# An encoder layer on one core: the first weight unit multiplied block by block over all token tiles, with constants and bias issued later

## The chip, the cores and the metric

The kernel runs on one core of one Trainium2 chip. The metric is the device time of one launch in microseconds (us), lower is better. It is the median of several runs of the same program.

## What is computed

The reference takes 768 tokens of width 1024 (256 of a prompt, 512 of a sample) through one encoder layer. The part that matters here is its beginning: a root-mean-square norm of the tokens, and one wide projection of the normed tokens into queries, keys, values and gates.

```python
def rms_norm(x, g):
    x32 = x.astype(jnp.float32)
    y = x32 * lax.rsqrt(jnp.mean(x32 * x32, axis=-1, keepdims=True) + EPS)
    return (y * g.astype(jnp.float32)).astype(x.dtype)

h = rms_norm(x, norm_g)
proj = h @ w_in
dq, dk, dv, nq, nk, nv, gates = jnp.split(proj, IN_SPLITS, axis=-1)
dq = rms_norm(dq.reshape(B, S, DIFF_HEADS, 2, DIFF_HEAD_DIM), diff_qn) * (DIFF_HEAD_DIM ** -0.5)
```

After it come differential attention, neighbourhood attention, a gated merge with an output projection, a second norm, and a mixture of 16 experts (each picks 96 tokens) whose weights make up most of the bytes that are read.

## The kernel before

**Tiles and stages.** The 768 tokens are 6 tiles of 128 (`t`, `NT = 6`), the width of 1024 is 8 blocks of 128 (`k`, `KD = 8`). The program goes through the stages one after the other: `pd` (projection to the differential attention's queries, keys, values), the attention itself, `pn` and its attention, `g` (gates and branches), `o` (output), the routing, the experts. A stage's projection is cut into chunks of 512 output columns (queries, keys, values for `pd`), and a chunk into weight units of 4 blocks by 512 columns, 1 MB each. The first chunk (queries) is units 0 and 1.

**High and low parts.** Every fp32 operand is split into a rounded part ("high", made by ACT) and the rest ("low", made by DVE), and every product is three matmuls (lines 492 to 494, `split_product`): high tokens by high weights, high tokens by low weights, low tokens by high weights. A unit takes 6 tiles x 4 blocks x 3 = 72 matmuls of 512 columns on PE.

**The start.** SP issues, in this order: tokens turned to blocks 0 to 3 (`xT`, two transfers of 768 KB, line 334), unit 0 (`w_raw`, 1 MB, line 330), blocks 4 to 7, unit 1, and then the tokens once more, not turned (`x`, six transfers of 512 KB, line 337). Meanwhile ACT's queue issues the vectors (`rows`: norm gains), the constants (`cst`: identity for the transposes, the exponents for the power) and the lambdas, and POOL's queue issues two tables of attention bias. ACT makes `hT_high` of each block (line 860) and `w_high` of each unit (line 851). DVE makes `hT_low` (line 1133) and `w_low` (line 1113). PE's first matmul waits for the first 4 token blocks, for the whole of unit 0, and for the constants.

**The norm.** The tokens go into the projection without their row norm, which is put on later. ACT squares and sums each row of `x` (line 867, six tiles), DVE makes the mean (line 1129), zeroes two key tiles (line 1142) and multiplies the lambda vectors (lines 1145 and 1148). ACT takes the exponent of the lambda sums (line 872) and only then enters the stage's body, where it first makes unit 2's `w_high`, then squares each projected tile (line 877). DVE makes unit 2's `w_low` before it reduces those squares (line 1160). POOL takes the power -0.5 (line 390) and DVE writes the scaled queries `qn` (line 1176).

**The order on PE.** It is written out: for each step (chunk, unit, tile) 12 matmuls, and two steps after a tile of queries or keys is complete, 4 transposes of it (line 501) that wait for its `qn`. Unit 1's tile 0 is the first complete one, so the first transposes stand behind unit 1's tile 2.

```python
                    while jt < len(done_at) and n >= done_at[jt] + 2:
                        if jt == 0 and before is not None:
                            pe.wait_ge(S(before, "out"), len(ATT[before]))
                        pe.wait_ge(S(stage, "qn"), jt + 1)
                        transposes(stage, jt, qn[:, jt % 2, :], "tr")
```

A unit's raw buffer, one of two, is loaded again once DVE has split it. ACT splits unit n once PE has finished unit n - 2.

Of the kernel before, what the change touches and what calls it, by code (L numbers as in the profile page):

```python
# [24 lines left out]
P = 128  # L25
# [3 lines left out]
NT = N // P  # L29
KD = D // P  # L30
# [23 lines left out]
ACT = mybir.ActivationFunctionType  # L54
# [59 lines left out]
def encoder(nc, x_prompt, x_sample, x_turned, w_in, vectors, lambdas, bias_diff, bias_prompt, bias_sample, w_branch_diff, w_branch_na,  # L114
            w_out, norm2_g, w_expert_gate, w_expert_up, w_expert_down, consts, y_prompt, y_sample):
    ctx = ExitStack()
    with ctx:
# [6 lines left out]
        def sem(name):  # L124
            return ctx.enter_context(nc.semaphore(name))
# [110 lines left out]
        s_x = [sem(f"x_loaded{t}") for t in range(NT)]  # L236
        s_xT = [sem(f"xT_loaded{i}") for i in range(4)]
        s_cst = sem("constants_loaded")
        s_lamv = sem("lambdas_loaded")
        s_kz = sem("keys_zeroed")  # L240
# [78 lines left out]
        def _(sp):  # L319
# [11 lines left out]

            for u in range(2):
                for i in (2 * u, 2 * u + 1):
                    sp.dma_start(xT[:, 2 * i:2 * i + 2, :], x_turned[:, 2 * i:2 * i + 2, :]).then_inc(s_xT[i], 16)
                load_unit(u, src_of("pd", "q", u))
            for t in range(NT):
# [39 lines left out]
        def _(pool):  # L376
            def load_bias(nh):
# [4 lines left out]
                pool.dma_start(BIAS[nh][4], BIAS[nh][3]).then_inc(s_b[b], 16)  # L382

            load_bias(0)
            load_bias(1)
            pool.wait_ge(s_cst, 32)

# [97 lines left out]
        def _(pe):  # L485
            mm = nc.tensor.matmul

            pe.sem_inc(x_used, SPLITS)
            pe.wait_ge(s_cst, 32)
            def split_product(out, sh, sl, mh, ml, first, last):  # L490
# [35 lines left out]
            def project(stage, before):  # L526

                chunks = [c for c in CHUNKS if c[0] == stage]
                steps = chunk_steps(chunks)
                def bank_free(c, t):  # L530
                    if c > 0:
                        pe.wait_ge(S(stage, "pused"), NT * (c - 1) + t + 1)
                    elif before is not None:
                        after_attention(before, t)
                    elif t == 0:
                        pe.wait_ge(S("n1", "tev"), 4)

                done_at, jt = [], 0
                for n, (c, u, t) in enumerate(steps):
                    if before is None and (c, u, t) == (0, 1, 0):  # L540
                        pe.wait_ge(S("n1", "tev"), KD)
                    if before is None or n >= START_EARLY:
                        chunk_product(chunks, c, u, t, hTh, hTl, bank_free)
                    if u == 1 and c < 2:
                        done_at.append(n)
# [5 lines that stand above are left out]
                        jt += 1  # L551
# [286 lines left out]
        def _(act):  # L838
# [3 lines left out]
            def split_units(upto):  # L842

                while unit[0] < min(upto, UNITS):
                    n = unit[0]
                    act.wait_ge(w_loaded[n % 2], 16 * (n // 2 + 1))
                    if n >= OUT + 2:
                        act.wait_ge(s_phd, 6)
                    elif n >= 2:
                        act.wait_ge(w_prod, NT * (n - 1))  # L850
                    a_(split_slot(n)[0], wraw[:, n % 2], ACT.Copy).then_inc(w_high, 1)  # L851
                    unit[0] += 1

            for dst, src in ((rows, vectors), (cst, consts)):
                act.dma_start(dst, src).then_inc(s_cst, 16)
            act.dma_start(lamv, lambdas).then_inc(s_lamv, 16)
            act.wait_ge(s_cst, 32)
            for k in range(KD):
                act.wait_ge(s_xT[k // 2], 16)
                a_(hTh[:, k, :], xT[:, k, :], ACT.Copy, scale=g1[:, k:k + 1]).then_inc(S("n1", "high"), 1)  # L860
                if k % 4 == 3:
                    split_units(k // 4 + 1)
            for t in range(NT):
# [237 lines left out]
        def _(dve):  # L1101
# [13 lines left out]
            def split_units(upto):  # L1115

                while unit[0] < min(upto, UNITS):
                    n = unit[0]
                    dve.wait_ge(w_high, n + 1)
                    high, lows = split_slot(n)  # L1120
                    low(lows, wraw[:, n % 2], high).then_inc(w_split, 1)
                    unit[0] += 1


            dve.sem_inc(x_split, RAWS - 1)
            dve.wait_ge(s_cst, 32)

# [3 lines left out]
            for k in range(KD):  # L1131
                dve.wait_ge(S("n1", "high"), k + 1)
                v.scalar_tensor_tensor(hTl[:, k, :], xT[:, k, :], g1[:, k:k + 1], hTh[:, k, :].bitcast(F32), ALU.mult,
                                       ALU.subtract).then_inc(S("n1", "tev"), 1)
                if k % 4 == 3:
                    split_units(k // 4 + 1)
            dve.wait_ge(S("n1", "sq"), NT)
# [3 lines left out]
            for r in range(2):  # L1141
                v.memset(kT[r][64 * (1 - r):64 * (2 - r)], 0.0).then_inc(s_kz, 1)
            dve.wait_ge(s_lamv, 16)
            for m in range(2):
# [449 lines left out]
```

## Time and profile before

| What | Before |
|---|---|
| Median of 3 runs | 2252.39 us (2251.98 to 2252.77) |
| Profiled execution, its own time | 2251.67 us |
| Span of its profile | 2249.9 us |
| PE busy | 2158.8 us, 96% of the span |
| DVE, ACT, POOL busy | 71%, 61%, 8% of the span |
| Bytes moved | 624 MB, 277 GB/s over the span |

The span is what the profile covers of one execution, from its first instruction to its last; the execution's own time is 1.8 us longer. Busy shares are averages over stages that have different limits: the experts, from about 750 us on, fill most of the span. A change of the first tens of microseconds has to be read in that stretch, by what each engine waits for there.

### The profile page before, as it was taken

The page shows a single profiled execution, that of the slowest core. Times are in us where ns is not written, and L with a number is a line of the kernel's source. Part 1 is how long each engine was busy: PE and PEld are TensorE (multiplying, and loading weights), DVE is VectorE, ACT ScalarE, POOL GpSimd, SP SyncE. Part 2 cuts the span into 40 slices and gives each one's busy share as a digit, 9 for nine tenths or more (in the row PEclk, how much of TensorE's full clock was granted, in tenths as well). Part 3 has the DMA queues.
Part 4 walks back from the last instruction along what each step waited for, and adds up shares of the span by engine and source line. Part 5 has one row for each costly group of instructions (what it writes and reads, how often), then busy time and mean ns, then how long its engine had stood idle before and what let it go on. Part 6 is the DMA issues. An engine that isn't in the chain of part 4 may idle for free.

```text
span 2249.9 us, 30606 instructions
## 1 busy us (share of the span) xinstructions
PE 2158.8 (96%) x11924; PEld 1878.6 (83%) x11924; DVE 1590.0 (71%) x1288; ACT 1379.6 (61%) x1118; POOL 183.4 (8%) x140
## 2 busy tenths in 40 slices
PE   6999979999995999999999999999999999999997
PEld 5867868888775998899988899898998989999896
DVE  5366334323437888888888888888888888888885
ACT  5365425222224777777777767777776777777774
POOL 2102200000013000010100101010010100101010
PEclk9999989999996999999999999999999999999999
DMA  5110142113415999999999999999999999999994
GB/s 228 58 54 26 38 137 73 61 70 113 162 57 202 358 376 361 375 371 374 367 374 372 369 375 372 368 376 362 381 369 366 383 352 382 367 374 371 366 379 173
DMA packets 71582, 623.99 MB, mean 277 GB/s; under 512 B 8336, under 2 KB 8720, under 8 KB 18800
## 3 DMA queue, kind: packets, MB, share of 16 engines
q1 hardware_dynamic: 63264, 595.62, 68.6%
q0 software_dynamic: 7840, 27.40, 4.3%
q8 instruction: 30, 0.49, 0.1%
q10 hardware_dynamic: 432, 0.34, 0.0%
q14 instruction: 16, 0.13, 0.0%
HBM read 609.70 MB, written 13.63 MB: 277 GB/s over the span
## 4 chain that ended last, share of the span: by engine, by line
PE 84%; DVE 5%; ACT 4%; issue 3%; DMA 3%; POOL 0%; SPq 0%; ACTq 0%; DVEq 0%; POOLq 0%
PE PS L492 26%; PE PS L494 26%; PE PS L493 26%; DVE x_w_low L1113 2%; ACT x_w_high L1046 2%; PE PS L573 2%; PE PS L832 1%; PE PS L588 1%; DMA bias_windows<-in_bias_prompt 1%; PE PS L501 1%; DMA w_raw<-in_w_in 1%; DVE hidden L1471 1%; PE PS L601 1%; ACT w_high L851 1%; PE PS L699 0%
## 5 line engine op out<-in xcount | busy, mean ns | idle before, releaser
L1113 DVE TENSOR_TENSOR x_w_low<-x_w_raw,x_w_high 128x2816 fp32r<-128x2816 f32 (+1 forms) x382 | 1176.7, 3090 | 243.7 <-ACT x_w_high L1046 242.3
L1046 ACT ACTIVATE x_w_high<-x_w_raw 128x2816 fp32r<-128x2816 f32 (+2 forms) x384 | 979.1, 2557 | 252.1 <-PE PS L494 207.0
L492 PE MATMUL PS<-x_w_high,xT_high 128*96 128x352 f32 x2048 | 667.4, 326 | 1.4 <-DVE xT_low L1113 1.4
L494 PE MATMUL PS<-x_w_high,xT_low 128*96 128x352 f32 x2048 | 660.2, 322 | 0.0
L493 PE MATMUL PS<-x_w_low,xT_high 128*96 128x352 f32 x2048 | 657.9, 321 | 0.0
L492 PEld LDWEIGHTS PS<-x_w_high,xT_high 128*96 128x96 f32 x2048 | 330.2, 161 | 6.8 <-issue 4.4
L493 PEld LDWEIGHTS PS<-x_w_low,xT_high 128*96 128x96 f32 x2048 | 332.5, 162 | 2.4
L494 PEld LDWEIGHTS PS<-x_w_high,xT_low 128*96 128x96 f32 x2048 | 331.7, 162 | 1.5
L492 PE MATMUL PS<-x_w_high,hidden_high 128*96 128x512 f32 x704 | 280.0, 398 | 2.3 <-DVE x_w_low L1113 1.0
L493 PE MATMUL PS<-x_w_low,hidden_high 128*96 128x512 f32 x704 | 278.2, 395 | 0.0
L494 PE MATMUL PS<-x_w_high,hidden_low 128*96 128x512 f32 x704 | 277.9, 395 | 0.0
L492 PE MATMUL PS<-w_high,hT_high 128*128 128x512 f32 x528 | 212.5, 402 | 17.1 <-DVE w_low L1113 17.1
L494 PE MATMUL PS<-w_high,hT_low 128*128 128x512 f32 x528 | 207.3, 393 | 0.0
L493 PE MATMUL PS<-w_low,hT_high 128*128 128x512 f32 x528 | 206.7, 392 | 0.0
L492 PEld LDWEIGHTS PS<-x_w_high,hidden_high 128*96 128x96 f32 x704 | 113.9, 162 | 55.6 <-issue 9.7
L851 ACT ACTIVATE w_high<-w_raw 128x2048 fp32r<-128x2048 f32 x26 | 49.7, 1913 | 175.4 <-PE PS L494 172.2
L1113 DVE TENSOR_TENSOR w_low<-w_raw,w_high 128x2048 fp32r<-128x2048 f32 x26 | 59.6, 2292 | 136.8 <-ACT w_high L851 136.5
L494 PEld LDWEIGHTS PS<-x_w_high,hidden_low 128*96 128x96 f32 x704 | 113.3, 161 | 47.9
L493 PEld LDWEIGHTS PS<-x_w_low,hidden_high 128*96 128x96 f32 x704 | 113.6, 161 | 43.5
L454 POOL DMA_INDIRECT gathered<-t_dram,idxi x17 | 44.8, 2635 | 1200.6 <-PE PS L778 1194.9
L492 PEld LDWEIGHTS PS<-w_high,hT_high 128*128 128x128 f32 x528 | 100.1, 190 | 36.0 <-issue 17.1
L494 PEld LDWEIGHTS PS<-w_high,hT_low 128*128 128x128 f32 x528 | 99.7, 189 | 21.8
(183 smaller groups left out, 1775.4 us busy)
## 6 DMA issues: line engine op xcount, KB each, us to landing
x_w_raw<-in_w_expert_gate SPq DMA_DIRECT2D x128, 1408.0 KB, 8.4
x_w_raw<-in_w_expert_up SPq DMA_DIRECT2D x128, 1408.0 KB, 8.9
x_w_raw<-in_w_expert_down SPq DMA_DIRECT2D x96, 1536.0 KB, 8.4
x_w_raw<-in_w_expert_down SPq DMA_DIRECT2D x32, 1024.0 KB, 7.0
w_raw<-in_w_in SPq DMA_DIRECT2D x20, 1024.0 KB, 4.8
x<-in_x_sample SPq DMA_DIRECT2D x8, 512.0 KB, 13.6
bias_windows<-in_bias_sample POOLq DMA_DIRECT2D x8, 512.0 KB, 3.9
w_raw<-in_w_out SPq DMA_DIRECT2D x4, 1024.0 KB, 5.0
```

Of the source, the lines that this page charges most:

```text
L454: pool.indirect_dma_start(xe, None, t_dram, bass.IndirectOffsetOnAxis(ap=idxi[:, col:col + 1], axis=0)).then_inc(S("x", "xe"), 16)
L492: mm(out, sh, mh, start=first, stop=False)
L493: mm(out, sh, ml, start=False, stop=False)
L494: return mm(out, sl, mh, start=False, stop=last)
L501: i = nc.tensor.transpose(PS[:, 6 + jt % 2, c * P:(c + 1) * P], src[:, c * P:(c + 1) * P], ident)
L573: i = mm(PS[:, nm * (step % ring) + m, 0:nt * P], queries, keys, start=True, stop=True)
L588: i = mm(PS[:, 6 + a % 2, 0:w], turned[:, a % 2, c * P:(c + 1) * P], values[:, h * w:(h + 1) * w], start=c == 0, stop=c == nt - 1)
L601: i = nc.tensor.transpose(PS[:, 4 + a % 2, c * P:(c + 1) * P], maps[:, a % 4, 0, c * P:(c + 1) * P], ident)
L832: i = nc.tensor.transpose(PS[:, 6 + u % 2, f * CAP:(f + 1) * CAP], hid[:, (f0 + f) * P:(f0 + f + 1) * P], ident[0:CAP, 0:CAP])
L851: a_(split_slot(n)[0], wraw[:, n % 2], ACT.Copy).then_inc(w_high, 1)
L1046: a_(xh[:, w % SPLITS, 0:n], xraw[:, w % RAWS, 0:n], ACT.Copy).then_inc(x_high, 1)
L1113: return v.tensor_tensor(out, src, high.bitcast(F32), ALU.subtract)
```

## The change

SP now issues the vectors first, then for each of the first four blocks one transfer of its tokens (384 KB) and one of its part of unit 0 (256 KB), then blocks 4 to 7, unit 1 and `x` as before. ACT and DVE split each of the four blocks as it arrives, tokens and weights in turn. PE multiplies unit 0 with the block as the outer loop and all 6 tiles inside, into 6 banks of PSUM; the 72 matmuls are the same ones. POOL issues the constants and lambdas once DVE has made the low part of block 3, and the two bias tables once it has made that of block 7. From unit 1 on, the program is as it was.

```diff
-            for u in range(2):
-                for i in (2 * u, 2 * u + 1):
-                    sp.dma_start(xT[:, 2 * i:2 * i + 2, :], x_turned[:, 2 * i:2 * i + 2, :]).then_inc(s_xT[i], 16)
-                load_unit(u, src_of("pd", "q", u))
+            sp.dma_start(rows, vectors).then_inc(s_rows, 16)
+            first = src_of("pd", "q", 0).rearrange("p (k c) -> p k c", k=4)
+            for k in range(4):
+                sp.dma_start(xT[:, k, :], x_turned[:, k, :]).then_inc(S("n1", f"xT_loaded{k}"), 16)
+                sp.dma_start(wraw[:, 0, k], first[:, k]).then_inc(S("n1", f"w_loaded{k}"), 16)
+            for i in range(2, 4):
+                sp.dma_start(xT[:, 2 * i:2 * i + 2, :], x_turned[:, 2 * i:2 * i + 2, :]).then_inc(s_xT[i], 16)
+            load_unit(1, src_of("pd", "q", 1))
...
+            pool.wait_ge(S("n1", "tev"), 4)
+            pool.dma_start(cst, consts).then_inc(s_cst, 16)
+            pool.dma_start(lamv, lambdas).then_inc(s_lamv, 16)
+            pool.wait_ge(S("n1", "tev"), KD)
             load_bias(0)
             load_bias(1)
-            pool.wait_ge(s_cst, 32)
+            pool.wait_ge(s_cst, 16)
...
-            pe.wait_ge(s_cst, 32)
...
-                    elif t == 0:
-                        pe.wait_ge(S("n1", "tev"), 4)
+
+                if before is None:
+
+                    for k in range(4):
+                        pe.wait_ge(S("n1", "tev"), k + 1)
+                        pe.wait_ge(S("n1", "w_low"), k + 1)
+                        for t in range(NT):
+                            i = split_product(PS[:, t, :], hTh[:, k, t * P:(t + 1) * P], hTl[:, k, t * P:(t + 1) * P],
+                                              wh[:, 0, k], wl[:, 0, k], k == 0, False)
+                            if k == 3:
+                                i.then_inc(w_prod, 1)
+                    pe.wait_ge(s_cst, 16)
...
-                    if before is None or n >= START_EARLY:
+                    if n >= (NT if before is None else START_EARLY):
                         chunk_product(chunks, c, u, t, hTh, hTl, bank_free)
...
-            for dst, src in ((rows, vectors), (cst, consts)):
-                act.dma_start(dst, src).then_inc(s_cst, 16)
-            act.dma_start(lamv, lambdas).then_inc(s_lamv, 16)
-            act.wait_ge(s_cst, 32)
+            act.wait_ge(s_rows, 16)
             for k in range(KD):
-                act.wait_ge(s_xT[k // 2], 16)
+                act.wait_ge(*((S("n1", f"xT_loaded{k}"), 16) if k < 4 else (s_xT[k // 2], 16)))
                 a_(hTh[:, k, :], xT[:, k, :], ACT.Copy, scale=g1[:, k:k + 1]).then_inc(S("n1", "high"), 1)
-                if k % 4 == 3:
-                    split_units(k // 4 + 1)
+                if k < 4:
+                    act.wait_ge(S("n1", f"w_loaded{k}"), 16)
+                    a_(wh[:, 0, k], wraw[:, 0, k], ACT.Copy).then_inc(S("n1", "w_high"), 1)
+            unit[0] = 1
+            split_units(2)
...
-                if k % 4 == 3:
-                    split_units(k // 4 + 1)
+                if k < 4:
+                    dve.wait_ge(S("n1", "w_high"), k + 1)
+                    low(wl[:, 0, k], wraw[:, 0, k], wh[:, 0, k]).then_inc(S("n1", "w_low"), 1)
+            dve.wait_ge(S("n1", "w_low"), 4)
+            dve.sem_inc(w_split, 1)
+            unit[0] = 1
+            split_units(2)
```

How the order moves, at three places. In these rows a name stands for a tile, `out<-in`, with the shape, and a wait is named by its semaphore.

On SP, the head of its queue (transfers in the order in which it issues them). Before:

```order
L334 DMA xT<-in_x_turned 128x1536 x2
L330 DMA w_raw<-in_w_in 128x2048
L334 DMA xT<-in_x_turned 128x1536 x2
L330 DMA w_raw<-in_w_in 128x2048
L337 DMA x<-in_x_prompt 128x1024 x2
L337 DMA x<-in_x_sample 128x1024 x4
```

And of the change:

```order
L333 DMA rows<-in_vectors 128x152
L336 DMA xT<-in_x_turned 128x768
L337 DMA w_raw<-in_w_in 128x512
L336 DMA xT<-in_x_turned 128x768
L337 DMA w_raw<-in_w_in 128x512
L336 DMA xT<-in_x_turned 128x768
L337 DMA w_raw<-in_w_in 128x512
L336 DMA xT<-in_x_turned 128x768
L337 DMA w_raw<-in_w_in 128x512
L339 DMA xT<-in_x_turned 128x1536 x2
L331 DMA w_raw<-in_w_in 128x2048
L342 DMA x<-in_x_prompt 128x1024 x2
```

The same bytes stand ahead of `x` on this queue, but for the vectors, which come new from ACT's queue.

On PE, the first unit. Before, one wait stands ahead of all 72 matmuls:

```order
L484 UNCONDITIONAL_BRANCH [waits barrier_Pool_Activation_PE_DVE_SP_release]
L492 MATMUL PS<-w_high,hT_high 128x512 [waits n1_tev,unit_split_ready,constants_loaded]
L493 MATMUL PS<-w_low,hT_high 128x512
L494 MATMUL PS<-w_high,hT_low 128x512
L492 MATMUL PS<-w_high,hT_high 128x512
```

In the change, such a wait stands ahead of every 18 matmuls (`n1_tev` counts low parts of token blocks, `n1_w_low` those of weight blocks); here the end of the first block and the start of the second:

```order
L502 MATMUL PS<-w_high,hT_low 128x512
L500 MATMUL PS<-w_high,hT_high 128x512
L501 MATMUL PS<-w_low,hT_high 128x512
L502 MATMUL PS<-w_high,hT_low 128x512
L500 MATMUL PS<-w_high,hT_high 128x512 [waits n1_w_low,n1_tev]
L501 MATMUL PS<-w_low,hT_high 128x512
```

The first matmul no longer waits for the constants nor for blocks 1 to 3.

On PE, the first transposes of queries (`cst` holds the identity), of the change:

```order
L500 MATMUL PS<-w_high,hT_high 128x512
L501 MATMUL PS<-w_low,hT_high 128x512
L502 MATMUL PS<-w_high,hT_low 128x512
L509 MATMUL PS<-cst,qn 128x128 [waits pd_qn]
L509 MATMUL PS<-cst,qn 128x128 x3
L500 MATMUL PS<-w_high,hT_high 128x512
L501 MATMUL PS<-w_low,hT_high 128x512
```

Before, the same rows stand at the same place, behind 108 matmuls (lines 492 to 494 and 501); nothing moved here.

## Rows read from the trace of the kernel before

**Rows 1.** The page's chain that ended last: shares of the span by engine.

```profile
PE 84%; DVE 5%; ACT 4%; issue 3%; DMA 3%; POOL 0%; SPq 0%; ACTq 0%; DVEq 0%; POOLq 0%
```

**Rows 2.** Waits of PE, 0 to 60 us: total us, times, longest us.

```profile
PE PS L492 <- DVE w_low L1113: 17.1, 1, 17.1
PE PS L501 <- DVE qn L1176: 0.3, 1, 0.3
```

**Rows 3.** The chain in order of time, 0 to 60 us: start us, us, what.

```profile
3.69 15.34 DMA w_raw<-in_w_in
19.05 1.92 ACT w_high L851
...
27.07 1.16 ACT junk L867 x2
...
29.12 2.62 DVE kT L1142
...
32.43 2.62 DVE kT L1142
...
35.78 1.91 ACT w_high L851
...
37.82 2.29 DVE w_low L1113
...
41.00 1.66 POOL small L390
...
42.69 0.76 DVE qn L1176
```

**Rows 4.** Timeline, 0 to 18 us: start, us, engine, line, what [idle before <-releaser].

```profile
5.46 1.28 ACT L860 ACT_TABLE_LOAD   x1 [5.46 <-DMA xT<-in_x_turned]
9.48 3.41 ACT L860 ACTIVATE hT_high<-xT,rows 128x768 fp32r<-128x768 f32 x4 [2.74 <-DMA cst<-in_consts]
10.54 3.80 DVE L1133 SCALAR_TENSOR_TENSOR hT_low<-xT,rows,hT_high 128x768 fp32r<-128x768 f32 x4 [10.54 <-ACT hT_high L860]
12.80 1.89 ACT L851 ACTIVATE w_high<-w_raw 128x2048 fp32r<-128x2048 f32 x1
...
14.73 2.29 DVE L1113 TENSOR_TENSOR w_low<-w_raw,w_high 128x2048 fp32r<-128x2048 f32 x1 [0.39 <-ACT w_high L851]
...
17.12 0.76 PE L492 MATMUL PS<-w_high,hT_high 128*128 128x512 f32 x1 [17.12 <-DVE w_low L1113]
```

**Rows 5.** Loads of `x` (line 337): issue durations ns, first and last issue; time to landing.

```profile
L337 SPq DMA_DIRECT2D x<-in_x_sample x4: 445/1252/2259, 5.2 to 8.5; - x4
L337 SPq DMA_DIRECT2D x<-in_x_prompt x2: 461/464/467, 4.2 to 4.7; - x2
...
DMA to landing us min/median/max: 16.1/17.9/19.2
```

**Rows 6.** The load of `x` issued last, at 8.5 us: KB, us to landing.

```profile
x<-in_x_sample SPq DMA_DIRECT2D x1, 512.0 KB, 18.2
```

**Rows 7.** All transfers between 2 and 27 us.

```profile
DMA packets 2371, 10.09 MB, mean 404 GB/s; under 512 B 272, under 2 KB 656, under 8 KB 2052
```

**Rows 8.** Timeline of PE at the first transposes of the `pd` stage.

```profile
43.49 0.65 PE L501 MATMUL PS<-cst,qn 128*128 128x128 f32 x4 [0.28 <-DVE qn L1176]
...
45.37 0.39 PE L492 MATMUL PS<-w_high,hT_high 128*128 128x512 f32 x1
```

**Rows 9.** Timeline of PE at the same place in the `pn` stage.

```profile
221.46 1.09 PE L501 MATMUL PS<-cst,qn 128*128 128x128 f32 x4 [3.08 <-DVE qn L1176]
...
224.88 0.39 PE L492 MATMUL PS<-w_high,hT_high 128*128 128x512 f32 x1
```

**Rows 10.** Stretches of 2 us: busy us by engine, granted TensorE clock, DMA share, GB/s.

```profile
221.00:223.00 2.00, 1.54 (x6) 1.47 (x7) 1.82 (x4) 0.41 (x1) 1.70 (x2) 0.60 0.60 250
...
225.00:227.00 2.00, 2.00 (x13) 1.65 (x12) 0.00 (x0) 0.54 (x1) 0.00 (x0) 1.00 0.04 8
```

**Rows 11.** A stretch in which `v_windows` loads (256 KB transfers, 2 KB pieces).

```profile
312.00:314.00 2.00, 0.90 (x3) 0.18 (x1) 0.13 (x1) 0.00 (x0) 0.00 (x0) 0.50 0.26 103
```

More of the change, by code:

```diff
@@ L236, in encoder @@
         s_x = [sem(f"x_loaded{t}") for t in range(NT)]
-        s_xT = [sem(f"xT_loaded{i}") for i in range(4)]
+        s_xT = {i: sem(f"xT_loaded{i}") for i in range(2, 4)}
         s_cst = sem("constants_loaded")
+        s_rows = sem("vectors_loaded")
         s_lamv = sem("lambdas_loaded")
@@ L845, in split_units @@
                     n = unit[0]
-                    act.wait_ge(w_loaded[n % 2], 16 * (n // 2 + 1))
+                    act.wait_ge(w_loaded[n % 2], 16 * ((n + 1) // 2))
                     if n >= OUT + 2:
@@ L1118, in split_units @@
                     n = unit[0]
-                    dve.wait_ge(w_high, n + 1)
+                    dve.wait_ge(w_high, n)
                     high, lows = split_slot(n)
@@ L1125, in _ @@
             dve.sem_inc(x_split, RAWS - 1)
-            dve.wait_ge(s_cst, 32)
+            dve.wait_ge(s_rows, 16)
             def mean_eps(out, in_, w, done):
@@ L1142, in _ @@
                 v.memset(kT[r][64 * (1 - r):64 * (2 - r)], 0.0).then_inc(s_kz, 1)
+            dve.wait_ge(s_cst, 16)
             dve.wait_ge(s_lamv, 16)
```

## The prediction

> **What bounds the kernel now.** I read the page's chain first: PE holds 84% of it [rows 1], so a start of PE that comes earlier shortens the whole run, as long as nothing else holds PE back afterwards. Then PE's waits in the first 60 us [rows 2]: there are only two, 17.1 us for the first weight unit's low part, and 0.3 us at the first transposes for the scaled queries `qn`. The first looks like the prize of this change. The second, small as it is, decides what the prize is worth, because it says that PE is not alone on the path at 43 us. So I read the chain in order of time [rows 3]: it does not run through PE's 26 us of matmuls at all. It runs from the load of unit 1 (landed at 19.05 us) to ACT's `w_high` of unit 1, six squares of `x` (the last starts at 27.07), two zeroings of key tiles on DVE (29.12 and 32.43), ACT's and DVE's split of unit 2 (35.78 and 37.82), POOL's power (41.00) and `qn` (42.69). Only then come the transposes, at 43.49 [rows 8]. Before the change, PE arrives 0.28 us ahead of that chain. The two are balanced almost to the microsecond, and the change speeds up only one of them.
>
> **PE's side.** Before, PE starts at 17.12 us, released by `w_low` [rows 4]. With blocks, it needs the first token and weight block alone. ACT's table load ended at 6.74 (5.46 + 1.28), and it hung on the first 768 KB of tokens, where now 384 KB and the vectors come first, so not later. Then a block's `hT_high` takes 3.41 / 4 = 0.85, its `hT_low` 3.80 / 4 = 0.95, and its `w_high` a quarter of 1.89, its `w_low` a quarter of 2.29 [rows 4] = 0.57. On the path lie 0.85, 0.95 and 0.57; `w_high`, 0.47, runs on ACT beside `hT_low`. PE starts at 6.74 + 2.37 = about 9.1 us, 8.0 us earlier.
>
> From start to transposes PE has 108 matmuls: 43.49 - 0.28 - 17.12 = 26.1 us, a slow start included [rows 4, 8]. A block of 18 is 4.3 us of that. It is fed in 384 + 256 KB at 404 GB/s [rows 7] = 1.6 us, and split in 1.3 us by ACT and 1.5 us by DVE, so the next block is always there. Unit 1 is needed 17.4 us after the start, at 26.5; even landing at 19.05 as before, with 1.92 and 2.29 behind it, it is ready by 23.3. So PE reaches the transposes at 9.1 + 26.1 = 35.2 us.
>
> **The norm's side.** What does the change do to `qn`? From the last square on, DVE's, ACT's and POOL's work is untouched and in the same order: 42.69 + 0.76 - 27.07 = 16.4 us [rows 3]. What could move is the squares. They need ACT free of unit 1's `w_high`, and `x`. ACT can be free earlier, since unit 1 lands earlier. But `x` cannot: the first of its six loads lands at 4.2 + 16.1 = 20.3, the last at 8.5 + 18.2 = 26.7 [rows 5, 6], 0.4 us before its square starts. The DMA engines are full all the way (404 GB/s over 2 to 27 us [rows 7]), and the bytes ahead of the last `x` tile stay the same: 5 MB of tokens and units, 3 MB of `x`, and the 1.3 MB of vectors, constants, lambdas and bias. All but the vectors POOL now issues in the middle of the stretch. Eight `hT_low` and four quarters of `w_low` take DVE 9.9 us from about 7.6, so the bias is issued near 17.5 and goes in between the tiles of `x`. So I take 0 for the move of `qn`, from the row it is nearest to, the landing of the last `x`.
>
> The bounds: if the bias slips behind `x` entirely, `x` comes 0.92 MB / 404 GB/s = 2.3 us earlier, and `qn` at most 2.3 + 0.4 = 2.7 us. In the other direction, pieces are shorter: 3 KB for token blocks, 2 KB for weight blocks, where 6 and 8 KB stood. `x` itself goes in 4 KB pieces at full rate [rows 5, 7]. The nearest row with 2 KB pieces is the load of `v_windows`, 103 GB/s [rows 11], though it reads another layout. If the 1.05 MB of weight blocks went at that rate, they would take 10.2 us and not 2.6, and `qn` would come 7.6 us late. I take the value near `x`.
>
> On this point the Trainium skill speaks against the change. The page DMA: Bandwidth & Descriptors, section Measured, says to batch transfers to 1 MiB or more for three quarters of the peak; its fit gives each transfer 2.0 us plus its bytes at 436 GB/s. By that, eight transfers of 384 and 256 KB cost 22 us where three larger ones cost 12, an estimate from that page, and the result would be some 10 us slower. The trace disagrees where transfers queue up: the six of 512 KB land 6.4 / 5 = 1.28 us apart [rows 5, 6], where the fit gives 3.2.
>
> **The other parts.** PE's wait for the constants now stands behind unit 0, at 26.5. They are issued when DVE has made four low parts, near 13.5, so nothing waits there. POOL's only other work in that time is the power at 41.00 [rows 3], and the bias is read in the attention, after all three chunks. The four extra waits on PE and the ten extra issues on SP (about 0.46 us each [rows 5]) cost nothing: SP is ahead of the DMA engines, which have work queued. If that cover were gone, ten issues would be 4.6 us.
>
> **What is late next.** PE reaches the transposes at 35.2 and waits to 43.5, 8.3 us, in place of 0.3. So the gain at the start is a wait at line 501, to the microsecond. And the wait has a price. In the `pn` stage PE already waits 3.08 us at the same line, and the granted clock is 0.60 of 2.4 GHz over the 2 us around the restart, that is 1.2 GHz for most of them, and 1.00 again from 225 us [rows 9, 10]. From the transposes' start to the seventh matmul behind them are 224.88 - 221.46 = 3.42 us there, and 45.37 - 43.49 = 1.88 us in `pd`, where PE had been busy [rows 8, 9]. The difference, 1.54 us, falls on PE just when PE is the bound again: it arrives at the second transposes later than their `qn`. Bounds: 0, if the clock is back by then, and 3.1, if it lasts twice as long.
>
> **The sum**, against the profiled execution: 2251.67 + 0 (move of `qn`) + 1.5 (clock) = 2253.2 us. That execution lies 0.7 us below the median, so the median goes to 2253.9 us, 0.07% more. A measurement of this kernel can tell about 0.2%, or 4.5 us, from no change. This is none.
>
> **The rivals.**
> - *The start counts in full.* If the transposes did not hold PE, the run would be 8.0 us shorter: 2244.4. For it speak the 17.1 us [rows 2] and PE's 84% [rows 1]; against it the chain [rows 3], which does not pass through PE before 43 us, and the unmoved order on PE. Chance 4%.
> - *The bias slips behind `x`.* `qn` 2.7 us earlier, clock lost: 2251.2, no change either. For it: POOL issues late. Against it: near 17.5 the last `x` tile is still 9 us off. 12%, inside the forecast's sign.
> - *The pieces are slow, and `x` comes late.* One mechanism, on the DMA queue of SP: the weight blocks at 103 GB/s push `x`, the squares and `qn` back 7.6 us, and with the clock the run is 9.1 us slower, 2261.5. It decides from 3.0 us on, when the 2.6 MB of the eight transfers take 9.5 us and not 6.5, a rate of 276 GB/s. For it: [rows 11]. Against: the full rate with `x` [rows 5, 7]. 8%. This is also the way in which the page's rule would work.
> - *The change doesn't do what it says*, PE not starting before some 15 us, since the blocks come in turn with other work. Then PE waits less at the transposes and keeps its clock: 2252.4. 6%.
>
> **How the numbers follow.** The forecast, the start's gain lost at the transposes, the norm's chain where it was, the clock paid: 70%. With the second and fourth rival, no measurable change has 0.88. Faster has the first rival and a little: 0.04. Slower has the third: 0.08. The range takes in the bounds of `qn` and the clock: from -2.7 + 1.5 = -1.2, and 1.0 less for a clock that costs less, 2250.2; up to 1.5 us of slower transfers with the long clock, +4.6, 2257.0. The far ends, 2244 and 2261, are left out.
>
> **What the profile after would show.** Right: PE's first matmul near 9 us; one wait of some 8 us of `L501`'s successor for `qn`, from about 35 to 43.5; a granted clock of about half in the 3 us behind it; the last square of `x` near 27, and the zeroings and `qn` where they were. Wrong: the last square before 24 or past 30, or transposes that start well before 43 us. The forecast falls if `x` lands at another time, or if PE's later stages give the time back.

## The result and the profile after

The changed kernel takes 2260.53 us (median of 6 runs, 2257.41 to 2262.31) where the kernel before takes 2252.47 us (6 runs). The ratio is 1.0032, 95% interval 1.0022 to 1.0042: 0.3% slower. On a second chip it was 1.0026 (1.0015 to 1.0036). I had forecast 2253.9 us and no measurable change.

The profiled execution took 2257.41 us, 5.7 us more than that of before. PE's waits in the first 60 us come first (total us, times, longest us):

```profile
PE PS L509 <- DVE qn L1200: 10.5, 1, 10.5
PE PS L500 <- DVE w_low L1131: 9.5, 1, 9.5
```

Line 509 is line 501 of before, where the wait was 0.3 us [rows 2]. PE starts at 9.5 us and not at 17.1, and all 7.6 us of that, and 2.6 more, are spent in front of the first transposes. The chain in order of time (start us, us, what) shows what it waits for:

```profile
10.27 19.39 DMA x<-in_x_sample
29.68 1.16 ACT junk L885 x2
...
31.73 2.62 DVE kT L1165
...
35.05 2.62 DVE kT L1165
...
38.40 1.90 ACT w_high L869
...
40.42 2.29 DVE w_low L1131
...
43.60 1.66 POOL small L399
...
45.28 0.76 DVE qn L1200
...
46.09 1.11 PE PS L509 x4
```

Against [rows 3] every step is there with its old duration, 2.6 us later. The chain now hangs on the last load of `x`, which lands at 29.66 us where it landed at 26.7 [rows 5, 6]. ACT waited for two tiles of `x` ahead of that (timeline of ACT, idle before and releaser at the end):

```profile
26.28 1.06 ACT L885 ACTIVATE junk<-x 128x1024 f32<-128x1024 f32 x1 [1.54 <-DMA x<-in_x_sample]
...
28.41 1.06 ACT L885 ACTIVATE junk<-x 128x1024 f32<-128x1024 f32 x1 [0.97 <-DMA x<-in_x_sample]
```

Then the clock, in stretches of 2 us (busy us by engine, granted clock, DMA share, GB/s):

```profile
44.00:46.00 2.00, 0.00 (x0) 0.00 (x0) 0.99 (x3) 0.30 (x1) 2.00 (x2) 0.50 0.85 319
46.00:48.00 2.00, 1.91 (x7) 1.72 (x8) 1.54 (x4) 0.69 (x1) 1.71 (x2) 0.50 0.41 172
48.00:50.00 2.00, 2.00 (x7) 1.53 (x6) 0.00 (x0) 0.00 (x0) 0.78 (x1) 0.51 0.00 0
50.00:52.00 2.00, 2.00 (x12) 1.69 (x11) 0.00 (x0) 0.66 (x2) 0.00 (x0) 1.00 0.00 0
```

PE works at 1.2 GHz for 3.9 us behind its wait. The same DVE instruction, compared in the two traces, is 2.6 us late before the transposes and 4.4 us late at 47.7 us of before (timelines of DVE, before and after):

```profile
47.66 0.69 DVE L1160 TENSOR_REDUCE small<-sq 128x8 f32<-128x512 f32 x1 [2.13 <-ACT sq L877]
```

```profile
52.06 0.69 DVE L1184 TENSOR_REDUCE small<-sq 128x8 f32<-128x512 f32 x1 [4.34 <-ACT sq L895]
```

The 1.8 us between are the clock. "Late at 47.7 us" stands for this comparison in what follows.

Why `x` lands late is in the first microseconds. The same view, in stretches of 1 us from 4 to 8 us, of before:

```profile
4.00:5.00 1.00, 0.00 (x0) 0.00 (x0) 0.00 (x0) 0.00 (x0) 0.00 (x0) 1.00 1.04 410
5.00:6.00 1.00, 0.00 (x0) 0.00 (x0) 0.00 (x0) 0.54 (x1) 0.00 (x0) 1.00 1.02 420
6.00:7.00 1.00, 0.00 (x0) 0.00 (x0) 0.00 (x0) 0.74 (x1) 0.00 (x0) 1.00 0.99 410
7.00:8.00 1.00, 0.00 (x0) 0.00 (x0) 0.00 (x0) 0.00 (x0) 0.00 (x0) 1.00 1.08 439
```

and after:

```profile
4.00:5.00 1.00, 0.00 (x0) 0.00 (x0) 0.00 (x0) 0.00 (x0) 0.00 (x0) 1.00 0.76 220
5.00:6.00 1.00, 0.00 (x0) 0.00 (x0) 0.00 (x0) 0.60 (x1) 0.00 (x0) 1.00 0.81 198
6.00:7.00 1.00, 0.00 (x0) 0.00 (x0) 0.00 (x0) 0.99 (x2) 0.00 (x0) 1.00 0.92 271
7.00:8.00 1.00, 0.00 (x0) 0.00 (x0) 0.25 (x1) 1.00 (x2) 0.00 (x0) 1.00 1.02 268
```

The engines are nearly as busy, and move little more than half as much. The trace's records of the single pieces say more. Of the 376 pieces of 2 and 3 KB in these 4 us, half take no more than 84 ns (2 KB) and 121 ns (3 KB), as between 8 and 12 us, where the rest of the eight transfers goes at 350 GB/s and more. But 61 of them take over twice that, together 20.8 of the 55.9 us that the 376 take on the 16 engines. Of the 235 pieces of 6 to 8 KB in the same 4 us of before, none does.

One more place lost time, far from the edit. POOL's 14 loads of bias windows in the neighbourhood attention run from the first to the last issue (timeline of POOL). Before:

```profile
307.74 0.60 POOL L382 DMA_DIRECT2D bias_windows<-in_bias_prompt  x1 [36.03 <-DVE small L1219]
...
363.97 0.53 POOL L382 DMA_DIRECT2D bias_windows<-in_bias_sample  x1 [3.67 <-DVE small L1219]
```

After:

```profile
310.47 0.60 POOL L387 DMA_DIRECT2D bias_windows<-in_bias_prompt  x1 [36.03 <-DVE small L1243]
...
368.05 0.53 POOL L387 DMA_DIRECT2D bias_windows<-in_bias_sample  x1 [3.67 <-DVE small L1243]
```

That is 56.2 us before and 57.6 after, though no instruction of it was changed.

### The profile page after: what moved, and what is told of

The parts are those of the page before. It is cut to its first block, busy times and chain, and to the rows that moved or that the text cites. A ratio compares the mean times of both kernels' runs of the same rounds, so it can differ in the third digit from the quotient of the medians.

```text
span 2255.6 us, 30622 instructions
## 1 busy us (share of the span) xinstructions
PE 2162.2 (96%) x11924; PEld 1881.6 (83%) x11924; DVE 1589.9 (70%) x1291; ACT 1380.4 (61%) x1121; POOL 181.6 (8%) x142
## 4 chain that ended last, share of the span: by engine, by line
PE 84%; DVE 5%; ACT 3%; issue 3%; DMA 3%; POOL 0%; SPq 0%; DVEq 0%; ACTq 0%; POOLq 0%
PE PS L500 26%; PE PS L502 26%; PE PS L501 25%; DVE x_w_low L1131 2%; ACT x_w_high L1064 2%; PE PS L591 2%; PE PS L606 1%; PE PS L850 1%; DMA x<-in_x_sample 1%; DMA bias_windows<-in_bias_prompt 1%; PE PS L509 1%; DVE hidden L1495 1%; PE PS L619 1%; DMA bias_windows<-in_bias_sample 0%; ACT w_high L869 0%
## 5 line engine op out<-in xcount | busy, mean ns | idle before, releaser
L1131 DVE TENSOR_TENSOR w_low<-w_raw,w_high 128x2048 fp32r<-128x2048 f32 (+1 forms) x29 | 60.1, 2071 | 137.8 <-ACT w_high L869 137.1
```

The costliest lines, as they stand in the source:

```text
L1131: return v.tensor_tensor(out, src, high.bitcast(F32), ALU.subtract)
```

## Experiments

Theory A: the small transfers run slow, so `x` and the norm's chain land late, and PE's long wait costs its clock. Theory B: the constants and bias, moved into the stretch of `x`, delay it. Theory C: the order by blocks costs PE time itself. All ratios are against the kernel before on the same chip, with their 95% intervals.

**The change again** (no edit).

> The changed kernel once more, on the chip of the next three. Both theories: 5 to 10 us over the kernel before; the last square of x near 29.7 us where it was 27.07, the first transposes near 46 us behind a wait of about 10 us, PE at half clock for some 3.8 us behind them. If the part of the loss that lies past 60 us is a matter of where the clock falls, the times scatter by some us and the granted clock of the runs goes with them.

Measured: 2259.74 us against 2253.07, ratio 1.0026 (1.0015 to 1.0036). Last square at 29.21, transposes at 45.63 behind a wait of 10.25 us, 4.1 us late at 47.7 us. The first 60 us repeat. The kernel before scattered from 2248.8 to 2257.1 us on this chip, so medians alone don't place a loss of 2 us. The profiles do.

**Three large transfers in place of eight.**

```diff
-            for k in range(4):
-                sp.dma_start(xT[:, k, :], x_turned[:, k, :]).then_inc(S("n1", f"xT_loaded{k}"), 16)
-                sp.dma_start(wraw[:, 0, k], first[:, k]).then_inc(S("n1", f"w_loaded{k}"), 16)
+            for i in range(2):
+                sp.dma_start(xT[:, 2 * i:2 * i + 2, :], x_turned[:, 2 * i:2 * i + 2, :]).then_inc(S("n1", f"xT_loaded{i}"), 16)
+            sp.dma_start(wraw[:, 0], first).then_inc(S("n1", "w_loaded0"), 16)
```

> The change with its first four blocks loaded in the three large transfers of before; everything else as changed. Theory A (the small transfers are slow in the first 9 us, so x and with it the norm land late): the last square of x starts at 27 to 27.5 again, the transposes at 43.5 to 44, and what is left over before is the clock, 1.5 to 2.5 us. Theory B (constants and bias, moved into the stretch of x, delay it): the last square stays near 29.7 and the time stays that of the change.

Measured: 2257.35 us, 1.0017 (1.0007 to 1.0027). The rate at 4 to 8 us is back (same view):

```profile
4.00:5.00 1.00, 0.00 (x0) 0.00 (x0) 0.00 (x0) 0.00 (x0) 0.00 (x0) 1.00 1.03 412
5.00:6.00 1.00, 0.00 (x0) 0.00 (x0) 0.00 (x0) 0.24 (x1) 0.00 (x0) 1.00 0.97 406
6.00:7.00 1.00, 0.00 (x0) 0.00 (x0) 0.00 (x0) 1.00 (x1) 0.00 (x0) 1.00 1.09 414
```

The last square and the transposes (timelines of ACT and PE):

```profile
26.34 1.06 ACT L885 ACTIVATE junk<-x 128x1024 f32<-128x1024 f32 x1
...
42.75 0.66 PE L509 MATMUL PS<-cst,qn 128*128 128x128 f32 x4 [4.16 <-DVE qn L1200]
```

Theory A holds, and B falls as a cause by itself: with constants and bias still issued late, the chain is even 0.7 us earlier than before. The 0.7 us are ACT's wait for unit 1, which lands at 16.7 us here and at 19.0 before (timelines of ACT, before and here, the squares right behind):

```profile
19.05 1.92 ACT L851 ACTIVATE w_high<-w_raw 128x2048 fp32r<-128x2048 f32 x1 [0.73 <-DMA w_raw<-in_w_in]
```

```profile
18.33 1.91 ACT L869 ACTIVATE w_high<-w_raw 128x2048 fp32r<-128x2048 f32 x1
```

At 47.7 us the kernel is 0.9 us late, which is the clock's 1.6 less that 0.7.

**Constants and bias at the start, small transfers kept.**

```diff
-            pool.wait_ge(S("n1", "tev"), 4)
-            pool.dma_start(cst, consts).then_inc(s_cst, 16)
-            pool.dma_start(lamv, lambdas).then_inc(s_lamv, 16)
-            pool.wait_ge(S("n1", "tev"), KD)
+            act.dma_start(cst, consts).then_inc(s_cst, 16)
+            act.dma_start(lamv, lambdas).then_inc(s_lamv, 16)
```

> The change with constants, lambdas and bias issued at the start, as before, and the small transfers kept. Theory A: the last square of x stays near 29 to 30.5 us, since the first microseconds carry the slow small transfers and the other bytes as well; time as the change within 1.5 us. Theory B: the last square comes back to about 27 us, transposes at 43.5, time 2.6 us under the change.

Measured: 2258.82 us, 1.0029 (1.0018 to 1.0041). Rates of 298, 257 and 277 GB/s between 5 and 8 us, last square at 29.64. A, against B. But here the squares wait for unit 1 and not for `x` (chain in order of time):

```profile
7.06 14.54 DMA w_raw<-in_w_in
21.62 1.92 ACT w_high L865
23.54 1.04 ACT junk L883 x2
```

Unit 1 lands 2.6 us later than before, and six squares follow without a gap. The slow transfers delay all that stands behind them on the queue, and whichever of unit 1 and `x` lands too late then holds the norm's chain.

**PE held back.**

```diff
+                    pe.wait_ge(S("n1", "tev"), KD)
                     for k in range(4):
```

> The change with PE held until all eight token blocks have their low part (about 19.4 us), so that it arrives at the transposes just when qn does. Theory A says that the wait of 10.5 us at the transposes costs its clock: with a wait of under 1.5 us PE keeps full clock there, and the run is about 1.8 us shorter than the change although PE starts 10 us later. Rival C (the order by blocks costs PE time itself, or an early start is worth something after all): the time is that of the change, or up to 9 us longer.

Measured: 2257.65 us, 1.0027 (1.0017 to 1.0037), which alone can't be told from the change. PE at the transposes, and the clock there (a stretch of 2 us):

```profile
46.36 0.66 PE L509 MATMUL PS<-cst,qn 128*128 128x128 f32 x4 [0.27 <-DVE qn L1201]
```

```profile
46.00:48.00 2.00, 1.73 (x10) 1.44 (x10) 1.42 (x4) 1.38 (x2) 1.30 (x2) 1.00 0.53 221
```

PE starts 10 us later than in the change, the transposes come 0.7 us later than in its repeat, and at 47.7 us the kernel is 2.9 us late and not 4.1. The early start is worth nothing, and the wait costs 1.9 us of clock. C falls.

**The small transfers alone, in the kernel before.** The same eight transfers, with PE's order, constants and bias as before.

> The kernel before with its first four token blocks and unit 0 loaded in the eight small transfers; order on PE, constants and bias as before. Theory A: 200 to 310 GB/s between 4 and 8 us where it was 410 to 440, last square of x near 29.5 to 30, transposes near 46, no wait over 1 us there, so no fall of the clock: 2.5 to 3.5 us slower in the first 60 us. If the pieces are not to blame: last square near 27, time as before. For the stretch from 300 to 365 us: longer by 1.3 us or more if five more transfers on SP's queue matter (as early_constants would have it, whose POOL list is that of before), as before within 0.3 us if only POOL's list does.

Measured: 2254.83 us against 2252.29, 1.0011 (1.0002 to 1.0021). 174 and 285 GB/s between 4 and 6 us, last square at 29.07, transposes at 46.44 with no wait for `qn`: PE itself started late, at 19.3, since unit 0 was late too. 2.9 us late at 47.7 us. The transfers account for 2.0 us of landing and 2.2 of PE's start. The rest is PE's slow pace behind its start: matmuls come 0.43 us apart for 5.5 us, before for 2.9, and 0.23 apart after that.

When the loads land, by kernel (issue plus time to landing, us; `late_on_pool` and `late_bias_on_before` are the kernel before with constants and bias, or the bias alone, issued late, see below):

| Kernel | Last load of the first four blocks | Unit 1 | Last `x` |
|---|---|---|---|
| before | 12.72 | 19.03 | 26.70 |
| the change | 12.72 | 19.18 | 29.66 |
| three large transfers | 10.43 | 16.67 | 25.37 |
| constants and bias at the start | 15.30 | 21.60 | 29.25 |
| small transfers on before | 14.76 | 21.03 | 28.71 |
| `late_on_pool` | 9.97 | 16.22 | 26.91 |
| `late_bias_on_before` | 10.45 | 16.71 | 25.24 |

So the eight transfers cost 2.0 us of landing in the kernel before, 2.3 us in the change, and 4.3 us at its last `x`. In the change this hides at first: constants and bias, 1.18 MB, no longer go along with the first loads, so unit 1 lands as before, and they come in between the tiles of `x` instead, from 20.2 to 28.1 us. Late constants and bias alone move the last `x` by 0.2 us, against B once more.

**The norm's chain made shorter.** DVE's zeroings and lambda products move ahead of the mean, into DVE's wait for the squares. Three kernels: in the kernel before, in the change, and in the change with three large transfers.

```diff
-            dve.wait_ge(S("n1", "sq"), NT)
-            mean_eps(nss, nss, D, S("n1", "ss"))
             dve.wait_ge(S("n1", "tev"), KD)
...
+            dve.wait_ge(S("n1", "sq"), NT)
+            mean_eps(nss, nss, D, S("n1", "ss"))
             dve.wait_ge(s_lae, 1)
```

> The kernel before with DVE's two zeroings and the lambda products moved ahead of the mean, into the time in which DVE waits for the squares of x. Theory (before the change PE and the norm's chain arrive at the first transposes together): the chain gets about 5 us shorter, PE's wait of 0.28 us goes, and nothing more: -0.3 us. Rival (the chain alone sets the end): 4 to 5 us faster.

> The same move in the changed kernel. Theory (the early start is lost in the wait for the norm's chain): PE's wait at the transposes falls from 10.5 us by 5 or more, down to what unit 2's late load leaves, transposes near 41 us; about 5 us faster than the change, so near or below the kernel before, with the clock still falling in a wait of over 3 us. Rival (the small transfers or the order by blocks cost PE time by themselves): no more than 1 us faster than the change.

> The changed kernel with the three large transfers and the shorter chain. Theory: last square near 26.5, the chain and PE both ready near 38 to 39 us, wait at the transposes under 1.5 us and full clock behind it: 4 to 5 us under the kernel before. Rival: as short_chain_after or the kernel before.

Measured, in this order: 0.9999 (0.9988 to 1.0010), 1.0007 (0.9998 to 1.0017), 0.9982 (0.9973 to 0.9992; 2250.19 us against 2252.79). The transposes of the three, one line each (timeline of PE; the first starts with no wait at all):

```profile
43.24 0.60 PE L501 MATMUL PS<-cst,qn 128*128 128x128 f32 x4
```

```profile
40.17 1.12 PE L509 MATMUL PS<-cst,qn 128*128 128x128 f32 x4 [4.82 <-DVE qn L1200]
```

```profile
39.35 0.66 PE L509 MATMUL PS<-cst,qn 128*128 128x128 f32 x4 [0.82 <-DVE qn L1200]
```

Shortening the chain alone gives 0.3 us, because PE then is the bound. Shortening it in the change takes 5.9 us off the transposes; at 47.7 us this kernel is 1.8 us ahead of before, with 1.5 us of clock lost behind its wait. With fast loads as well 4.1 us are gained at 47.7 us.

**The stretch from 300 to 365 us.** Eight kernels asked which part of the change lengthens it. Theory D, one more transfer on SP's queue shifts it, was the first guess.

> The kernel before once more, with a second profile. If what the change loses past 60 us is a matter of where the clock's falls land, this profile too differs from the first one there by 1 to 3 us, with the first 60 us alike (last square near 27, transposes at 43.5). If it is the change's own doing, the stretch from 60 us to the end is as in the first profile within 0.5 us, and no fall of the clock shows near 600 us.

> The kernel before with the vectors alone moved from ACT's queue to the head of SP's. In all profiles of kernels with the change's loads, the stretch from 300 to 365 us (neighbourhood attention, waiting for its bias windows) is 1.3 to 3.5 us longer than in all three profiles with the loads of before. Theory D (one more transfer on SP's queue shifts how later transfers of SP and POOL share the DMA engines): here too the stretch is 1.3 us or more longer, the first 60 us as before within 0.5 us. Rival: stretch as before within 0.3 us.

> The kernel before with constants, lambdas and bias issued late by POOL as in the change, the vectors still on ACT's queue, SP's transfers and PE's order as before. Theory B once more (late constants delay x): last square 2 us late. Theory A: last square near 26.5 to 27.1, PE starts some us earlier (no wait for constants), waits for qn at the transposes, time within 2 us of before. For the stretch from 300 to 365 us: rival of D (two more transfers on POOL's queue shift it) 1.3 us or more longer; D: as before.

> The version with three large transfers and the shorter chain, with the vectors issued by ACT's queue, so that SP's list of transfers is that of before. First 60 us as in short_chain_big (transposes near 39.4). Theory D: the stretch from 300 to 365 us is back to that of before, and the time is about 2 us under short_chain_big, 5 to 6 us under the kernel before. Rival (POOL's list or anything else): the stretch stays 1.3 us or more longer, time as short_chain_big.

> The version with three large transfers and the shorter chain, with vectors, constants and lambdas on ACT's queue at the start, so that the lists of transfers of both SP and POOL are those of before (the bias still issued late). First 60 us as in short_chain_rows_act, at most 0.7 us later (transposes 38.8 to 39.6). If POOL's two extra transfers make the stretch from 300 to 365 us longer (as late_on_pool says), it is back to that of before within 0.3 us here, and the median is 5 to 7 us under the kernel before and 2 to 4 us under short_chain_rows_act. Rival (the late bias or the order of the units does it): the stretch stays 1.3 us or more longer, time as short_chain_rows_act.

> The kernel before with unit 0 multiplied block by block on PE, started at the same time and with the same loads as before. First 60 us as before within 0.5 us by every theory but C. For the stretch from 300 to 365 us: 1.3 us or more longer if the order on PE brings the loss there (as early_constants has it, whose bias is as early as before), else as before within 0.3 us.

> The kernel before with only the two bias tables issued late by POOL, constants as before. First 60 us: PE starts 1 to 3 us earlier and waits for qn, transposes 42.5 to 44. For the stretch from 300 to 365 us: 1.3 us or more longer if the late bias brings the loss there (as short_chain_lists has it, whose lists are those of before), else as before within 0.3 us.

> The version with three large transfers, the shorter chain and both lists as before, with the bias at the start as well. First 60 us: PE starts 1 to 2 us later than in short_chain_lists, transposes at 39.5 to 41.5, 2 to 4 us under before. The stretch from 300 to 365 us: as before within 0.3 us if the late bias is what lengthens it, 1.3 us or more longer if the order on PE does.

The edits: `rows_on_sp` issues the vectors from SP; `late_on_pool` takes the change's lines for POOL into the kernel before; `late_bias_on_before` takes only the wait ahead of the bias; `block_order_on_before` takes only the loop by blocks on PE; the three others stand in their expectations. Time from the first to the last of the 14 issues, worked out from the timelines of POOL, and the ratios:

| Kernel | 14 issues, us | Ratio (95%) |
|---|---|---|
| before, and again | 56.2, 56.3 | 0.9998 (0.9988 to 1.0007) |
| short chain before | 56.1 | above |
| vectors on SP | 56.5 | 1.0002 (0.9993 to 1.0012) |
| small transfers on before | 56.3 | above |
| block order on before | 56.2 | 1.0001 (0.9991 to 1.0012) |
| late bias on before | 57.9 | 1.0001 (0.9992 to 1.0011) |
| late constants and bias on before | 60.0 | 1.0005 (0.9996 to 1.0015) |
| the change, and again | 57.6, 59.6 | above |
| held start; three large transfers; early constants | 59.6; 59.7; 59.3 | above |
| short chain: after; big | 59.5; 57.7 | above |
| short chain, vectors on ACT | 59.8 | 0.9988 (0.9978 to 0.9997) |
| short chain, both lists as before | 57.7 | 0.9987 (0.9978 to 0.9997) |
| short chain, all issued at the start | 57.6 | 1.0001 (0.9990 to 1.0011) |

The stretch takes one of three lengths, near 56.3, 57.7 and 59.6 us. But one program gives two of them, the change 57.6 and its repeat 59.6, and only two programs were profiled twice. Theory D falls (vectors on SP, small transfers on before). The order on PE alone does nothing either. Late bias alone is enough, with 1.7 us in its profile, and late constants with it had 3.8; that the constants make the difference is not shown:

```profile
302.89 0.60 POOL L382 DMA_DIRECT2D bias_windows<-in_bias_prompt  x1 [36.05 <-DVE small L1220]
...
360.79 0.53 POOL L382 DMA_DIRECT2D bias_windows<-in_bias_sample  x1 [3.67 <-DVE small L1220]
```

```profile
307.54 0.60 POOL L383 DMA_DIRECT2D bias_windows<-in_bias_prompt  x1 [36.03 <-DVE small L1223]
...
367.52 0.53 POOL L383 DMA_DIRECT2D bias_windows<-in_bias_sample  x1 [3.67 <-DVE small L1223]
```

But two kernels with an early bias have it too (`early_constants`, `short_chain_early`), so lateness is one way there and not the only one. In both, PE starts by 14.2 us and ACT and DVE split unit 0 block by block; which of these counts was not separated. Nor do the ratios of the kernel before with a late bias, alone or with the constants, show a loss clear of noise. In the change's repeat DVE waits 4.1 us at once for a window of the sample, in the second profile of before 2.5 us in two waits. So it is in how these loads land. Through what the first transfers act on loads 300 us later stays open.

Two expectations for the first 60 us missed. With all issued at the start, unit 1 lands at 19.0 us again and the transposes come at 41.69, not by 41.5. And the late bias alone did more than I thought: I expected a wait for `qn` and transposes at 42.5 to 44; but without the bias ahead of them unit 0 and `x` land earlier (table above), so PE's side and the norm's chain both move. PE starts at 15.46 us and transposes without a wait:

```profile
41.68 0.66 PE L502 MATMUL PS<-cst,qn 128*128 128x128 f32 x4
```

That is 1.8 us gained in the first 60 from one added wait, in a profile whose stretch at 300 us then loses 1.7. The times do not tell it from the kernel before (1.0001).

The second profile of before also says how far single profiles can be compared past 60 us. The first 60 us and the stretch above are as in the first, and yet it ends 2.4 us later: 1.2 us at 130 us and 1.6 us near 600 us, both at falls of the clock that the first profile had shorter or not at all.

**The version that beats both.** Three large transfers, shorter chain, early start: 0.9982 (0.9973 to 0.9992), and with SP's and POOL's lists as before, the bias still late, 0.9987 (0.9978 to 0.9997), 2248.15 us against 2252.29. Both are 0.1 to 0.2% faster than the kernel before, about the bound of what can be told here.

## Why the prediction was wrong

- **PE's side: right.** Start at 9.5 us (9.1 forecast), arrival at the transposes at 46.09 - 10.48 = 35.6 (35.2). The wait stood at the very line that was named, 10.5 us and not 8.3, and `held_start` showed that the whole early start is lost there.
- **The clock: right in kind, 1.8 us where I took 1.5.** With no wait it vanishes.
- **The move of `qn`: this step failed.** I took 0; it was +2.6 us. The bytes ahead of `x` did stay the same and the engines were busy, as I argued. But I took the rate from the transfers of `x` [rows 5, 7], and the eight small ones did not run at it: 198 to 271 GB/s between 4 and 8 us. Large transfers in their place bring the last square from 29.68 to 26.34 us, so the eight transfers cost 3.3 us there, and 2.0 in the kernel before. The third rival named the slow transfers, with 8%, and priced them at 7.6 us from `v_windows` [rows 11]. I misread that row: its DMA engines are 0.26 busy, so it shows that few bytes were asked for, and not what a 2 KB piece costs. Nor is the size of the pieces alone the cause, since between 9 and 10 us the same transfers run at 412 GB/s. No row of before had this load at the head of the queue, and the price should have been left open.
- **The rule of the Trainium skill.** The Trainium skill, DMA: Bandwidth & Descriptors, section Measured, asks for large transfers; by its fit the loss would have been some 10 us, an estimate. The trace agrees in sign, with 2.0 to 3.3 us, a third of that or less. That section of the Trainium skill measured transfers issued from GpSimd, and these are SP's. I had set the rule aside because the six loads of `x` queue up at full rate. They do, and it says nothing of pieces at the start.
- **"The other parts" cost nothing: this failed too.** The late constants and bias wait for nobody where they are read, but the stretch at 300 us got 1.4 us (profile) to 3.4 us (repeat) longer. `late_on_pool` shows 3.8 us of that kind from this part alone, with its first 300 us within 0.2 us of before. That is read from the profiles: in its time, 1.0005 (0.9996 to 1.0015), it is not clear of no change.
- **The sum.** 2.6 and 1.8 us in the first 60, 1.4 to 3.4 us at 300, make 5.8 to 7.8 us. The medians say 8.1 and, on the second chip, 6.7. In the profiled execution falls of the clock elsewhere almost cancel (1.6 us less at 220 us, 1.4 more near 600). They come and go between runs of one program.
- **The rivals.** The start did not count in full, as forecast. The range, up to 2257.0, was too narrow because it allowed 1.5 us for slow transfers between bounds of 0 and 7.6, and nothing for a place that was not edited.

## What to carry to other kernels

An engine's early start is worth what the next join leaves of it: find the chain that arrives there at the same time, and shorten both, or neither pays. A transfer cut into pieces must be priced by a row with the same piece and layout at the same place in the queue; without such a row the price is open, and the range has to say so. A low rate is the price of a piece only where the DMA engines are busy. Moving transfers in time can lengthen a stretch where nothing was edited, so compare the traces stretch by stretch over the whole span before a loss is put down to the edit.

## What was not expected of the hardware

- Eight transfers of 384 and 256 KB at the head of the queue ran at 198 to 271 GB/s for four microseconds, with the DMA engines 0.76 to 1.02 busy, and the rest of the same eight, from 8 us to their end at 12.7, at 350 to 412 GB/s and more. The change's repeat (249 to 308 GB/s over the same four), the change with early constants (257 to 298 over 5 to 8 us, after 420) and the small transfers on the kernel before (174 and 285 over 4 to 6 us, then 378 and more) did so too. The two kernels with large transfers whose rates are told here, the one before and the change with three, did not. A sixth of the pieces in these four microseconds takes over twice the usual time. What holds them up is not shown, nor whether the number, the size or the alternation of the eight transfers does it.
- The stretch at 300 us took 56.1 to 56.5 us in six profiles of five kernels and 57.6 to 60.0 in the twelve profiles of the other eleven. Each of the eleven issues the bias late or starts PE by 14.2 us, and none of the five does. The change gave both 57.6 and 59.6.
- A fall of the clock cost 1.2 to 1.9 us where PE was the bound, and whether it happens differs between two profiles of the same program.
